# Last attention's tail: another order of its instructions, and one more PSUM bank for head 6

## What is computed

```
q, k = rope(rms(q)), rope(rms(k))           # 8 heads, 2 halves of 64 each
s = einsum('bqhad,bkhad->bhaqk', q, k) * scale
p = softmax(s)                              # over 512 keys: context and tokens
a = p[:, :, 0] - lam * p[:, :, 1]           # the mixed map of a head
o = einsum('bhqk,bkhe->bqhe', a, v)         # [256, 8, 128]
o = _rms(o, subln_w) * (1.0 - lam_init)     # norm over the 128 of a head
out = o.reshape(...) @ w_out                # 1024 x 1024
```

## Time and profile before

| what | us |
|---|---|
| median of 3 runs | 2168.42 (2165.92 to 2171.74) |
| the profiled execution, its time | 2165.16 |
| its span in the profile | 2163.7 |
| PE busy | 2036.8 (94%) |
| DVE, ACT, POOL busy | 1386.5, 1014.6, 423.0 |

### The profile page before, as it was taken

One profiled execution on the slowest core, in us unless ns is written; L12 is line 12 of the kernel. 1 busy time (PEld: TensorE's weight loads), 2 busy tenths in 40 slices (PEclk: granted clock), 3 DMA queues, 4 the chain that ended last, 5 costly groups with the idle time before them and its releaser, 6 DMA issues.

```text
span 2163.7 us, 32246 instructions
## 1 busy us (share of the span) xinstructions
PE 2036.8 (94%) x12804; PEld 1687.1 (78%) x12804; DVE 1386.5 (64%) x2299; ACT 1014.6 (47%) x1810; POOL 423.0 (20%) x308
## 2 busy tenths in 40 slices
PE   7999999999999899999999999999999999969999
PEld 4776677888987786999975447788898777648999
DVE  4394657867968656655555345786797855546555
ACT  3444644432543556544553353453354355535443
POOL 1000317412521004100100331751352100000000
PEclk9999999999999999999999999999999999989999
DMA  9641521548458535456634002154732822114564
GB/s 340 209 152 59 175 79 59 191 132 272 137 187 292 161 98 195 156 167 197 183 117 156 1 3 95 59 190 144 251 98 69 277 70 68 59 39 137 161 210 118
DMA packets 276742, 311.62 MB, mean 144 GB/s; under 512 B 6128, under 2 KB 260208, under 8 KB 269424
## 3 DMA queue, kind: packets, MB, share of 16 engines
q1 hardware_dynamic: 271888, 304.90, 43.2%
q10 hardware_dynamic: 4704, 4.65, 0.7%
HBM read 308.48 MB, written 1.05 MB: 143 GB/s over the span
## 4 chain that ended last, share of the span: by engine, by line
PE 70%; DVE 15%; ACT 7%; DMA 3%; POOL 3%; issue 3%; ACTq 0%; SPq 0%; DVEq 0%; POOLq 0%
PE bank L779 69%; DVE weights_low L1566 3%; ACT weights_high L2365 1%; DVE weights_low L1947 1%; DMA modulation_slots<-p_modulation_rows 1%; DVE scratch L1558 1%; DVE yT L1558 1%; DVE modulation_slots L1592 1%; DVE input_low L1558 1%; PE bank L788 1%; DMA parameter_columns<-p_columns 1%; DVE xT L1558 1%; DVE big L1558 1%; DVE hidden_low L1961 1%; DVE big L2090 0%
## 5 line engine op out<-in xcount | busy, mean ns | idle before, releaser
L779 PE MATMUL bank<-input_high,weights_high 128*128 128x256 f32 (+1 forms) x2336 | 751.0, 323 | 26.7 <-DVE scratch L1985 9.4
L779 PE MATMUL bank<-input_high,weights_low 128*128 128x256 f32 (+1 forms) x2336 | 737.1, 317 | 0.0
L779 PE MATMUL bank<-input_low,weights_high 128*128 128x256 f32 (+1 forms) x2336 | 716.2, 318 | 5.3 <-DVE input_low L1558 5.2
L779 PEld LDWEIGHTS bank<-input_high,weights_high 128*128 128x128 f32 x2336 | 441.5, 189 | 87.3 <-issue 29.8
L1566 DVE TENSOR_TENSOR weights_low<-weight_slots,weights_high 128x1024 fp32r<-128x1024 f32 (+2 forms) x344 | 384.7, 1157 | 185.2 <-ACT weights_high L2365 184.9
L779 PEld LDWEIGHTS bank<-input_low,weights_high 128*128 128x128 f32 x2336 | 435.4, 189 | 43.2 <-DVE input_low L1558 9.8
L779 PEld LDWEIGHTS bank<-input_high,weights_low 128*128 128x128 f32 x2336 | 441.5, 189 | 33.5
L2365 ACT ACTIVATE weights_high<-weight_slots 128x1024 fp32r<-128x1024 f32 (+2 forms) x348 | 314.3, 950 | 149.9 <-PE bank L779 136.5
L1947 DVE TENSOR_TENSOR weights_low<-weight_slots,weights_high 128x512 fp32r<-128x512 f32 x216 | 233.1, 1098 | 33.9 <-ACT weights_high L2643 31.9
L779 PE MATMUL bank<-hidden_high,weights_high 128*128 128x256 f32 (+1 forms) x704 | 238.6, 339 | 1.2 <-DVE weights_low L1566 0.9
L779 PE MATMUL bank<-hidden_low,weights_high 128*128 128x256 f32 (+1 forms) x704 | 237.3, 337 | 0.0
(11 more groups left out here) (284 smaller groups left out, 2776.6 us busy)
## 6 DMA issues: line engine op xcount, KB each, us to landing
weight_slots<-w_gu SPq DMA_DIRECT2D x44, 1024.0 KB, 5.1
weight_slots<-ffn_w_in SPq DMA_DIRECT2D x44, 1024.0 KB, 5.1
modulation_slots<-p_modulation_rows SPq DMA_DIRECT2D x64, 512.0 KB, 4.9
modulation_slots<-mod_w SPq DMA_DIRECT2D x32, 1024.0 KB, 6.6
modulation_slots<-w_mod SPq DMA_DIRECT2D x28, 1024.0 KB, 6.6
weight_slots<-w_in SPq DMA_DIRECT2D x24, 1024.0 KB, 8.1
weight_slots<-w_down SPq DMA_DIRECT2D x16, 768.0 KB, 5.0
weight_slots<-ffn_w_out SPq DMA_DIRECT2D x16, 768.0 KB, 5.9
```

Source lines behind the costliest of these rows:

```text
L779: return pe.matmul(o, w, r, start=start, stop=stop, skip_group_check=shared)
```

## The change

In layer 3's attention:

- Tables: product of head 4 goes from step 23 to 22, of head 5 from 24 to 23; score pair 15 and the turnings 13 to 15 leave the tables and are written out in `odd_mixer`, as are the products of heads 6 and 7.
- Head 6's product goes to bank 4, where the values of the heads are turned; it waits for the last of those to be copied away. Heads 4, 5 and 7 stay in bank 7. Head 7 waits for head 5's copy.
- On ACT, `odd_step` does the exponentials ahead of the copy of a turned map, in all steps of the projection too.
- The norm of heads 0 to 3 goes forward: means at step 21 (was 22), bounds on DVE and the root with its two table loads on ACT at step 22, the factors on DVE at step 23, the first spread on PE after step 23. All three of spreads 0 to 2 now use bank 5, and spreads 1 and 2 wait for the multiplications that read it.
- In the tail each program has a new order; both `upper_mixed` pieces come after all products and means, one ahead of spreads 2 and 3 and one behind them; the weights of output item 1 are split in halves at two places.

```diff
-SCORES = {6: 0, 7: 1, 8: 2, 9: 3, 10: 4, 11: 5, 12: 6, 13: 7, 16: 8, 17: 9, 18: 10, 19: 11, 21: 12, 22: 13, 23: 14, 24: 15}
-FLIPS = {e + 2: x for e, x in SCORES.items()}
-PRODUCTS = {11: 0, 12: 1, 17: 2, 18: 3, 23: 4, 24: 5, 25: 6, 27: 7}
+SCORES = {6: 0, 7: 1, 8: 2, 9: 3, 10: 4, 11: 5, 12: 6, 13: 7, 16: 8, 17: 9, 18: 10, 19: 11, 21: 12, 22: 13, 23: 14}
+FLIPS = {e + 2: x for e, x in SCORES.items() if e < 22}
+PRODUCTS = {11: 0, 12: 1, 17: 2, 18: 3, 22: 4, 23: 5}
...
-        return self.bank[4 if h < 4 else 7][:, X]
+        return self.bank[4 if h < 4 or h == 6 else 7][:, X]
...
     def odd_product(h):
-        if h:
-            pe.wait_ge(*m.odd_join.at(0, h - 1))
+        if h in (1, 2, 3, 5, 7):
+            pe.wait_ge(*m.odd_join.at(0, h - (2 if h == 7 else 1)))
...
     def sub_spread(u):
+        if u in (1, 2):
+            pe.wait_ge(*m.odd_y.at(0, 2 * u - 1))
...
     def odd_projection(L):                       # PE
-            if e == 22:
+            if e == 21:
                 pe.wait_ge(*m.head_root.end(L))
                 for h in range(4):
                     sub_mean(h)
+            if e == 23:
+                sub_spread(0)
     def odd_mixer(L):                            # PE
-        odd_step(24)
-        odd_step(25)
-        for u in range(2):
-            sub_spread(u)
-        odd_step(26)
+        odd_scores(15)
+        odd_flip(13)
+        sub_spread(1)
+        odd_product(6)
+        odd_flip(14)
         for h in (4, 5):
             sub_mean(h)
+        odd_flip(15)
+        odd_product(7)
+        for h in (6, 7):
+            sub_mean(h)
         upper_mixed(L, 0)
-        odd_step(27)
-        sub_mean(6)
-        upper_mixed(L, 1)
-        sub_mean(7)
         pe.wait_ge(*m.odd_keyed.end(0))
         for u in (2, 3):
             sub_spread(u)
+        upper_mixed(L, 1)
...
     def odd_projection(L):                       # DVE
             coming_weights(L, e)
+            if e in (22, 23):
+                sub_norm(0, (e - 22,))
...
-        sub_norm(0, range(1))
     def odd_mixer(L):                            # DVE
         odd_projection(L)
+        odd_normalised(0)
+        to_tokens(L, 7, m.od_v[:, 7, :, :], 4)
+        odd_joined(5)
+        sub_bounded(4)
+        odd_maximum(15)
         odd_mix(14)
-        to_tokens(L, 7, m.od_v[:, 7, :, :], 4)
-        odd_step(24)
+        odd_low(0)
+        odd_normalised(1)
         odd_reciprocals(15)
-        sub_norm(0, range(1, 2))
+        sub_bounded(5)
         odd_mix(15)
-        odd_step(25)
-        sub_bounded(4)
-        for u in range(2):
-            odd_normalised(u)
-        odd_step(26)
-        sub_bounded(5)
-        next_weights(m.outp[L][0])
+        odd_joined(6)
+        odd_low(1)
+        low_weights(m.outp[L][1], range(1))
         sub_bounded(6)
-        odd_step(28)
+        odd_joined(7)
         sub_bounded(7)
         sub_norm(1)
+        low_weights(m.outp[L][1], range(1, 2))
         for u in (2, 3):
             odd_normalised(u)
+            odd_low(u)
...
     def odd_step(e):                             # ACT
+        if e in SCORES:
+            odd_exponential(SCORES[e])
         if e in FLIPS:
             odd_keys(FLIPS[e])
         if e in SCORES:
-            odd_exponential(SCORES[e])
             odd_second(SCORES[e])
     def odd_projection(L):                       # ACT
+            if e == 22:
+                sub_root(0)
+                ln_exp_tables()
     def odd_mixer(L):                            # ACT
-        odd_step(24)
-        sub_root(0)
-        ln_exp_tables()
-        odd_step(25)
-        sub_square(4)
-        for u in range(2):
-            odd_cut(u)
-        odd_step(26)
+        odd_keys(13)
+        odd_exponential(15)
+        odd_cut(0)
+        odd_second(15)
         sub_square(5)
-        next_weights(m.outp[L][0])
+        odd_keys(14)
+        odd_cut(1)
+        odd_keys(15)
+        high_weights(m.outp[L][1], range(1))
         sub_square(6)
         sub_square(7)
         sub_root(1)
+        high_weights(m.outp[L][1], range(1, 2))
```

More of the change, by code:

```diff
@@ L1445, in odd_product @@
     def odd_product(h):
-        pe.wait_ge(*m.v_tokens.at(3, h | 1 if h < 4 else h))
+        pe.wait_ge(*m.v_tokens.at(3, h | 1 if h < 4 or h == 6 else h))
         pe.wait_ge(*m.odd_keyed.at(0, 2 * h + 1))
@@ L1465, in sub_spread @@
         pe.wait_ge(*m.sub_v.at(0, 5 * (u // 2) + 4))
+        if u in (1, 2):
+            pe.wait_ge(*m.odd_y.at(0, 2 * u - 1))
         for t in range(2):
             q = 32 * (2 * (u % 2) + t)
-            i = mm(bank[(5, 0, 5, 6)[u]][:, t * SEQ:(t + 1) * SEQ], ident[:, q:q + 1].to_broadcast([P, P]), m.sub_ms, True, True)
+            i = mm(bank[(5, 5, 5, 6)[u]][:, t * SEQ:(t + 1) * SEQ], ident[:, q:q + 1].to_broadcast([P, P]), m.sub_ms, True, True)
         i.then_inc(m.sub_spread.sem, 1)
@@ L2259, in sub_factors, with odd_normalised @@
         tt(ms, ms, ok, ALU.mult).then_inc(m.sub_v.sem, 1)
-    def odd_normalised(u, L=3):
+    def odd_normalised(u):
         dve.wait_ge(*m.sub_spread.at(0, u))
@@ L2264, in odd_normalised, with odd_low @@
             h = 2 * u + t
-            muladd(m.od_o[:, h, :], m.od_o[:, h, :], m.lams[:, 6:7], bank[(5, 0, 5, 6)[u]][:, t * SEQ:(t + 1) * SEQ], ALU.mult,
+            muladd(m.od_o[:, h, :], m.od_o[:, h, :], m.lams[:, 6:7], bank[(5, 5, 5, 6)[u]][:, t * SEQ:(t + 1) * SEQ], ALU.mult,
                    ALU.mult).then_inc(m.odd_y.sem, 1)
+    def odd_low(u, L=3):
         for h in (2 * u, 2 * u + 1):
```

## The result

| | before | changed |
|---|---|---|
| median us | 2169.59 (4 runs, 2165.92 to 2171.74) | 2151.86 (4 runs, 2149.87 to 2155.71) |
| ratio, 95% interval | | 0.9921 [0.9906, 0.9937] |
| profiled execution, its span | 2165.16, 2163.7 | 2149.87, 2148.4 |

Faster by 0.8%; forecast was 2152.0. The page of the changed kernel shows the same work as the earlier trace rows, and the windows show where it now waits less. The columns are those of the earlier trace rows.

A forecast was written before the change was run, and what follows sets the result against it. PE was taken to wait in the tail, 18.1 us idle from 1903 to 1951, in a ring of small steps over PE, ACT and DVE. The second output tile added at 1939.2 instead of 1955.35 gave 16.2 us less, 2152; range 2147 to 2162.

The forecast's parts named there:

- Product 4 ahead of tile 23: End of the projection, PE full: the product's 1.83 us only delay tile 23, ending at 1904.3 instead of 1902.45.
- The root hidden, no slack: ACT, last projection steps: root and two table loads, 3.0 us, end just when tile 23 must be copied.
- The drain: Rival, ACT's table switches: each adds about 1380 ns, leaving 14.2 us gained, 2154.2; chance 0.05.
- Exponentials 15, low parts, mixing 15: First part of tail: exponentials start at 1913.1, low parts end 1915.8, mixing ends 1919.25 instead of 1923.2.
- new wait: Tail, DVE: low parts 0 and 1 wait for ACT's high parts, 0.84 us, queued behind exponentials 15.
- This is what the second bank buys.: Tail, PE: turning 15 comes 11 us earlier, the largest piece, since product 6 runs beside exponentials 15.
- Product 6 with no bracket: Sign of being right, tail of PE's timeline: product 6 shows no wait for DVE's copy.
- Check of the method: The same sum over the old order fell 2 us short at spread 2; 1.2 added for the shorter tail.
- Exponentials and turned maps in the projection: Swap on ACT in 12 projection steps: costs nothing given 1.15 us of slack, bound 0 to 1 us in all.
- The clock did not stay down: Rival, tail: PE stays at half clock behind waits, leaving 8.4 us gained, 2160.0; chance 0.20.
- The other chain: Rival, tail: another chain binds, likely DVE's added work, leaving 4.9 us gained, 2163.5; chance 0.08.
- the slower rival: Rival, projection: late DVE shifts hold up turned maps in 12 steps, PE waits for bank 6, 2176; chance 0.04.

The follow-up runs named there:

- c_low_later: Changed kernel with low and high parts of heads 0 to 3 moved later and square and bound 5 ahead of mixing 15: 2144.81 us, ratio 0.9891.
- a_one_bank: Changed kernel with head 6's product put back in bank 7, waiting for the copy of head 5's product: 2147.36 us, ratio 0.9896.
- b_exp_first: Kernel before, with only ACT's exponentials put ahead of the copy of a turned map: 2162.61 us, ratio 0.9968.
- b_norm_early: Kernel before, with only the lower heads' means, bounds, root and factors moved forward, spreads left in place: 2167.17 us, ratio 0.9991.
- a_keys_first: Changed kernel with ACT again copying the turned map ahead of the exponentials in the projection steps: 2151.49 us, ratio 0.9914.
- c_products_later: c_low_later with products 1 and 3 moved one step later in the projection, against that kernel's 2144.81: 2145.94 us, ratio 0.9884.
- d_simple: c_products_later with head 6's product back in bank 7, so no second bank: 2143.32 us, ratio 0.9888.
- a_busy: Changed kernel with twelve 128x128 matmuls, results unread, filling PE's two waits ahead of product 7: 2148.29 us, ratio 0.9895.

## Why the prediction was right or wrong

**The forecast.** 2152.0 against 2151.86, and 16.2 us against 17.7 in the stretch it was worked out for. That the median came out so close is partly luck: 1.5 us of gain too little met a median of the kernel before that stood 1.2 lower with three runs than with four. The profiled execution, forecast at 2149.0 and measured at 2149.87, has luck in it too: the stretch ahead came out 2.3 us longer.

**Product 4 ahead of tile 23: +1.83.** Right. From head 4's turned values to the last ones it takes 17.89 us, was 15.97: +1.92.

**The root hidden, no slack.** Right, to the hundredth. The copy of tile 23 starts 0.26 us behind the start of PE's next turning (1906.81, 1907.07); before, it was 0.26 too (1902.45, 1902.71). The second load ended at 1907.05.

**The drain (Trainium skill, ScalarE: Activation LUTs, "What ACT_TABLE_LOAD costs").** Not seen. The load starts 0.02 us behind the second map's end (1903.30 + 0.72, 1904.04), the root 0.01 behind the load, and the whole takes 3.0 us. By that rule the two switches would have moved the copy to about 1909.8, 2 x 1.38 later; it stood at 1907.07.

**Exponentials 15, low parts, mixing 15.** I shift my times by the 2.51 us by which the last turned values came later than in my sum (1906.81, not 1904.3), scatter and all. Exponentials 15: 1915.6 forecast, 1915.90 measured. Mixing 15 ends: 1921.8, measured 1921.55. Turning 15: 1921.9, measured 1921.60. Product 7: 1923.1, measured 1922.99, at 3.64 instead of 3.75. Spread 2: 1932.8, measured 1932.47, at full clock. So the chain of the forecast is the one that binds, with its new wait; c_low_later shows the price of that order, 3.1 us, with what it costs in clock. One small wait I had not: product 5 waits 0.61 for the copy of head 4 (1908.52), behind the factors' 1.75 us reciprocal on DVE.

**"This is what the second bank buys."** Wrong, and the worst step of the text. I computed when turning 15 comes and then gave the whole difference to one of several causes. The bank is worth nothing in the changed kernel (51.10 without it, 51.15 with it), and 5.9 alone in the old. The order of DVE's copy does the same (5.2 alone). The rest of turning 15's 11 us has several sources, the factors and the root no longer ahead of mixing 15 and the earlier exponentials among them; how it divides was not measured. The sum stayed right since it never used the bank: in my own times product 6 starts after copy 5. "Product 6 with no bracket" could then not tell right from wrong; a_one_bank has none either.

**"Check of the method": +1.2.** Wrong. From the last turned values to the second tile added it took 33.26 us (1940.07 - 1906.81). My sum without the correction gives 33.7 (1938.0 - 1904.3), with it 34.9. The sum over the old order fell 2 us short; perhaps through that order's slow clock (0.85 over its tail, 0.97 now), but that wasn't tested. Without the correction the forecast gain would have been 17.4.

**Exponentials and turned maps in the projection: 0.** Right: 122.58 against 122.44, and 122.3 to 122.7 with and without the swap.

**The rivals.** The clock did not stay down: 0.70 from 1924 to 1928 in product 7, then 1.00. The page section I weighed (Trainium skill, TensorE: Matmul & The Clock Gate, "A second HAM failure mode") names falls and rises between groups of matmuls: the trace agrees for one fall in the changed tail, 1.5 us in size, not for a tail at half clock. The other chain and the slower rival did not come: no turning between 1780 and 1900 has a bracket.

**Open.** Why the stretch of equal instructions ahead scatters by 7 us. Most of it is PE's busy time on the same matmuls: 1666.9 us in the shortest (b_exp_first, 1761.93) and 1672.8 in the longest (b_norm_early, 1768.85), with 95.0 and 96.0 of idle time. The granted clock goes with it. The four kernels above 1768 have 0.91 to 0.93 from 200 to 300, all others 0.97 to 1.00; the next two (1767.52, 1767.05) have 0.93 from 1100 to 1200, all others 0.98 to 1.00. What lowers it in one execution and not in another stays open. The rest takes 210.1 us instead of 208.4 in two kernels, all of it in PE's busy time (205.3 and 205.1 instead of 203.4) at a granted clock that reads 1.00 in every one, so the clock in the records doesn't explain that. What else is in the projection's two stalls, 5.7 us of idle time still, wasn't tried.

## What to carry to other kernels

Where engines run in written order and PE waits for a copy, look at what stands in front of the copy on its engine before spending a buffer on it: another place in the order alone gave 5.2 us where the bank alone gave 5.9, and in the final order the bank added nothing. Undo the parts of a change one at a time as well as doing them alone; 16.7 us of single gains for a whole of 17.7 looked like four separate parts, and one of them was worth nothing once the others were there. For effects of a few us in a kernel of 2150, cut the profile at marks and compare stretches, since equal code alone scattered by 7 us.

## What the runs showed of the hardware

- Product 7, the same eight records, took 3.61 to 3.75 us in three kernels (changed, a_one_bank, a_keys_first) behind waits of 2.8 to 2.9 and 0.73, and 1.97 in three (c_low_later, c_products_later, d_simple) behind 1.20 to 1.25 and 0.73, or with the longer waits filled by idle matmuls (a_busy). The idle time just before is not the whole of it: product 5 took 3.02, 3.07 and 3.75 us in three kernels behind the same 1.59 and 1.94.
- An extra 12 matmuls 128x128 that compute nothing made the tail 1.5 us shorter.
- A switch of ACT's table cost its load of 1.28 us with 0.01 to 0.02 us on either side: of the 3.03 us from 1904.04 to 1907.07, the two loads are 2.56 and the root between them 0.42.
